# Hidden activations of an expert block: DRAM scratch and 32x32 turns on VectorE in place of transposes on TensorE

## The reference

```python
hid = jax.nn.silu(xb @ w1[e]) * (xb @ w3[e])   # xb: 128 rows of 1024, w1/w3: 1024 x 512
return hid @ w2[e]                             # w2: 512 x 1024
```

## Time and profile before

| | us |
|---|---|
| runs: median (lowest to highest of 3) | 1350.07 (1349.74 to 1353.28) |
| profiled execution: span from first to last instruction | 1348.3 |
| TensorE busy | 1311.4 |
| VectorE busy | 958.4 |
| GpSimd busy | 525.1 |
| ScalarE busy | 511.7 |

### The profile page before, as it was taken

One profiled execution on the slowest core, in us unless ns is written; L12 is line 12 of the kernel. 1 busy time (PEld: TensorE's weight loads), 2 busy tenths in 40 slices (PEclk: granted clock), 3 DMA queues, 4 the chain that ended last, 5 costly groups with the idle time before them and its releaser, 6 DMA issues. The chain is left out here.

```text
span 1348.3 us, 20368 instructions
## 1 busy us (share of the span) xinstructions
PE 1311.4 (97%) x6382; PEld 1095.8 (81%) x6383; DVE 958.4 (71%) x1357; ACT 511.7 (38%) x568; POOL 525.1 (39%) x543
## 2 busy tenths in 40 slices
PE   5999999999999999998999999999999999999995
PEld 5888888888888888887888888888888888888884
DVE  7758577687759785698777886665675677776564
ACT  3423234322443234323444454343443454434241
POOL 2001010111101110022566665755665656666555
PEclk9999999999999999999999999999999999999998
DMA  9625434563455344544777774563554545666421
GB/s 266 181 89 162 149 111 163 170 192 109 156 186 158 110 141 159 208 181 169 287 263 256 271 270 147 193 234 132 181 202 181 191 164 214 236 231 238 142 69 64
DMA packets 156522, 243.58 MB, mean 181 GB/s; under 512 B 18944, under 2 KB 84992, under 8 KB 156480
## 3 DMA queue, kind: packets, MB, share of 16 engines
q1 hardware_dynamic: 118624, 154.15, 35.3%
q0 software_dynamic: 28928, 71.74, 15.0%
q10 hardware_dynamic: 8928, 17.13, 3.7%
HBM read 211.97 MB, written 64.62 MB: 205 GB/s over the span
## 5 line engine op out<-in xcount | busy, mean ns | idle before, releaser
L520 PE MATMUL acc<-ring_hi 128*128 128x512 f32 (+1 forms) x800 | 308.8, 386 | 2.1 <-DVE ring_lo L1239 1.9
L522 PE MATMUL acc<-ring_hi,ring_lo 128*128 128x512 f32 (+1 forms) x800 | 305.6, 382 | 0.0
L521 PE MATMUL acc<-ring_lo,ring_hi 128*128 128x512 f32 (+1 forms) x800 | 305.3, 382 | 0.0
L520 PE MATMUL acc<-ring_hi,xt_hi 128*128 128x512 f32 x648 | 256.7, 396 | 4.1 <-issue 2.8
L522 PE MATMUL acc<-ring_hi,xt_lo 128*128 128x512 f32 x648 | 252.8, 390 | 0.0
L521 PE MATMUL acc<-ring_lo,xt_hi 128*128 128x512 f32 x648 | 252.4, 390 | 0.0
L1802 POOL TENSOR_TENSOR small<-small 128x1 f32<-128x1 f32 x31 | 47.4, 1527 | 360.8 <-DVE small L1208 360.8
L520 PEld LDWEIGHTS acc<-ring_hi 128*128 128x128 f32 x800 | 151.3, 189 | 30.1 <-DVE ring_lo L1239 2.5
L522 PEld LDWEIGHTS acc<-ring_hi,ring_lo 128*128 128x128 f32 x800 | 151.2, 189 | 29.1
L521 PEld LDWEIGHTS acc<-ring_lo,ring_hi 128*128 128x128 f32 x800 | 151.3, 189 | 27.7
L921 ACT CAST ring_hi<-stage_x 128x2048 fp32r<-128x2048 f32 x64 | 119.4, 1915 | 76.3 <-PE acc L522 75.8
(11 more groups left out here) (276 smaller groups left out, 1884.0 us busy)
## 6 DMA issues: line engine op xcount, KB each, us to landing
stage_x<-in_exp_w SPq DMA_DIRECT2D x64, 1024.0 KB, 6.2
stage<-in_w_in SPq DMA_DIRECT2D x64, 512.0 KB, 5.4
stage<-in_exp_w SPq DMA_DIRECT2D x32, 1024.0 KB, 6.6
stage<-in_w_out SPq DMA_DIRECT2D x32, 512.0 KB, 5.3
h_scratch<-hres POOLq DMA_DIRECT2D x16, 512.0 KB, 3.0
sum_scratch<-hres ACTq DMA_DIRECT2D x16, 512.0 KB, 2.9
hrow<-in_x POOLq DMA_DIRECT2D x12, 512.0 KB, 4.8
h_scratch<-hrow POOLq DMA_DIRECT2D x12, 512.0 KB, 3.0
```

Of the source, the lines that this page charges most:

```text
L520: nc.tensor.matmul(dst, w_hi, x_hi, start=start, stop=False)
L521: nc.tensor.matmul(dst, w_hi, x_lo, start=False, stop=False)
L522: return nc.tensor.matmul(dst, w_lo, x_hi, start=False, stop=stop)
```

## The change

`hid_tile` is no longer called for the blocks 1 to nb - 2; the first block and the last keep it. In its place `hid` goes to DRAM and comes back with the 32-column strips of its rows rearranged to partitions: quarter a of `hid_q` holds the columns 128a to 128a + 127 of all 128 rows, 32 rows on the partitions and four groups of rows side by side. VectorE's `transpose` then turns each 32x32 block of `hid_q` into `aux`. The partition 32a + c of slice k then holds column 128a + 32k + c, so w2 is loaded in that order of rows (`w2_v`), with four DMAs for each unit, and the first and the last block, which TensorE still transposes, write `hid` in the same order by four strided pieces (`by_tile`). ScalarE issues the store (`hid_out`) after `x_hi` and ahead of the w3 copies, and the four reads (`hid_back`) after them. `silu(b)` and `hid_hi(b - 1)` change places on ScalarE; VectorE's turn stands at the head of its block, ahead of `hid_lo`.

```diff
-    w2_v = exp_w2[0].rearrange("(g i) (k p) n -> i g p k n", p=P, g=NEG)
+    w2_v = exp_w2[0].rearrange("(g i) (a k c) n -> i g a c k n", a=QUARTERS, c=SUB, g=NEG)
+    hid_dram = nc.dram_tensor("hid_scratch", (P, DE), F32).ap()
+    hid_quarters = hid_dram.rearrange("(b r) (a f) -> a r b f", r=SUB, a=QUARTERS)
...
+                    for a in range(QUARTERS):
+                        src = w2_v[ex // NEG, ex % NEG, a, :, (j % 2) * 2:(j % 2 + 1) * 2, :]
+                        dst = staged(j)[a * SUB:(a + 1) * SUB, 0, :].rearrange("p (k c) -> p k c", k=2)
+                        sp.dma_start(dst, src).then_inc(s_stage[j], 16)
...
-            pe.wait_ge(s_plist, 1)
-            hid_tile(1)
...
                 down(pe_of)
-                hid_tile(b)
...
+            def hid_out(b):
+                act.wait_ge(s_hid, b + 1)
+                act.wait_ge(s_hq, b * 16 * QUARTERS)
+                act.dma_start(hid_dram, hid[:]).then_inc(s_hst, 16)
+            def hid_back(b):
+                act.wait_ge(s_hst, b * 16 + 16)
+                for a in range(QUARTERS):
+                    act.dma_start(hid_q[a * SUB:(a + 1) * SUB, :].rearrange("r (b f) -> r b f", f=P), hid_quarters[a])\
+                        .then_inc(s_hq, 16)
             def hid_hi(b):
-                act.wait_ge(s_htr, b + 1)
+                if isinstance(b, int) and b == 0:
+                    act.wait_ge(s_htr, 1)
+                else:
+                    act.wait_ge(s_hturn, b + 1)
...
+                    silu(b)
                     hid_hi(b - 1)
-                    silu(b)
...
                 x_hi(b + 1)
+                hid_out(b)
                 with act.If(ends > 0):
                     if first:
                         split_hi_expert(e_of + 1, 1)
                     units_hi(e_of + 1, 1)
+                hid_back(b)
...
-                if not (isinstance(b, int) and b == 0):
-                    dve.wait_ge(s_htr, b)
+                if isinstance(b, int) and b == 1:
+                    dve.wait_ge(s_htr, 1)
+                elif not (isinstance(b, int) and b == 0):
+                    dve.wait_ge(s_hst, b * 16)
...
+            def hid_turn(b):
+                dve.wait_ge(s_hq, b * 16 * QUARTERS)
+                V.transpose(aux[:].rearrange("p (k b c) -> p k b c", k=FT, c=SUB),
+                            hid_q[:].rearrange("p (b k c) -> p k b c", k=FT, c=SUB)).then_inc(s_hturn, 1)
...
-                    if split:
-                        hid_lo(b - 1)
+                    hid_turn(b)
+                    hid_lo(b - 1)
```

More of the change, by code:

```diff
@@ L64 @@
 ROW = D + NE
+SUB = 32
+QUARTERS = P // SUB
 ALIGN = 128
@@ L288, in build @@
         hid = e("hid", [P, DE])
+        hid_q = e("hid_q", [P, DE])
         ht_hi = e("ht_hi", [P, FT, P], F32R)
@@ L422, in build @@
         s_htr = sem("hid_transposed")
+        s_hst = sem("hid_rows_stored")
+        s_hq = sem("hid_quarters_in")
+        s_hturn = sem("hid_quarters_turned")
         s_hthi = sem("hid_t_hi")
@@ L491, in load_expert @@
             def load_expert(ex, j):
-                v = (w1_v, w3_v, w2_v)[j // 2]
-                kts = v.shape[3] // 2
-                src = v[ex // NEG, ex % NEG, :, (j % 2) * kts:(j % 2 + 1) * kts, :]
-                dst = staged(j)[:, 0, :].rearrange("p (k c) -> p k c", k=kts)
-                sp.dma_start(dst, src).then_inc(s_stage[j], 16)
+                if j < 4:
+                    v = (w1_v, w3_v)[j // 2]
+                    src = v[ex // NEG, ex % NEG, :, (j % 2) * 4:(j % 2 + 1) * 4, :]
+                    dst = staged(j)[:, 0, :].rearrange("p (k c) -> p k c", k=4)
+                    sp.dma_start(dst, src).then_inc(s_stage[j], 16)
[3 more added lines that the diff above has]
+                        dst = staged(j)[a * SUB:(a + 1) * SUB, 0, :].rearrange("p (k c) -> p k c", k=2)
+                        sp.dma_start(dst, src).then_inc(s_stage[j], 16)
             for j in (0, 1, 4, 2, 3, 5):
@@ L918, in split_hi_expert @@
             def split_hi_expert(ex, j):
-                act.wait_ge(s_stage[j], (ex + 1) * 16 + (MU // 2 * 32 if j < 2 else 0))
+                act.wait_ge(s_stage[j], (ex + 1) * (16 if j < 4 else 16 * QUARTERS) + (MU // 2 * 32 if j < 2 else 0))
                 nc.scalar.copy(ring_hi[:, j:j + 1, :], staged(j)).then_inc(s_ehi[j // 2], 1)
@@ L1160, in _ @@
                 act.wait_ge(s_ahout[t], 16 * NCH)
+            act.sem_inc(s_hst, 16)
+            act.sem_inc(s_hq, 16 * QUARTERS)
             silu(0)
@@ L1410, in route_hots @@
                                         lists[:, 0, 1:2], ALU.add).then_inc(s_gn, 1)
-                        hid_rows(0)
+                        hid_rows(0, True)
                     for t in range(TPC):
@@ L1571, in x_lo, with hid_rows @@
                                     ALU.subtract).then_inc(s_xtlo, 1)
-            def hid_rows(b):
+            def hid_rows(b, by_tile=False):
                 dve.wait_ge(s_silu, b + 1)
                 dve.wait_ge(s_w3, b + 1)
-                if not (isinstance(b, int) and b == 0):
-                    dve.wait_ge(s_htr, b)
+                if isinstance(b, int) and b == 1:
+                    dve.wait_ge(s_htr, 1)
+                elif not (isinstance(b, int) and b == 0):
+                    dve.wait_ge(s_hst, b * 16)
                 dve.wait_ge(s_gcol, b + 1)
                 col = gate_0 if isinstance(b, int) and b == 0 else gate[:, bass.ds(b, 1)]
-                V.scalar_tensor_tensor(out=hid[:], in0=act_a[:], scalar=col, in1=acc[1][:], op0=ALU.mult,
-                                       op1=ALU.mult).then_inc(s_hid, 1)
+                if by_tile:
+                    tiles = hid[:].rearrange("p (k a c) -> p a k c", k=FT, c=SUB)
+                    parts = [(tiles[:, a], *(t[:, a * P:(a + 1) * P].rearrange("p (k c) -> p k c", c=SUB)
+                                             for t in (act_a, acc[1]))) for a in range(QUARTERS)]
+                else:
+                    parts = [(hid[:], act_a[:], acc[1][:])]
+                for to, x_a, x_b in parts:
+                    ins = V.scalar_tensor_tensor(out=to, in0=x_a, scalar=col, in1=x_b, op0=ALU.mult, op1=ALU.mult)
+                ins.then_inc(s_hid, 1)
+            def hid_turn(b):
+                dve.wait_ge(s_hq, b * 16 * QUARTERS)
+                V.transpose(aux[:].rearrange("p (k b c) -> p k b c", k=FT, c=SUB),
+                            hid_q[:].rearrange("p (b k c) -> p k b c", k=FT, c=SUB)).then_inc(s_hturn, 1)
             def hid_lo(b):
@@ L1712, in final_last, with turn @@
                                        op0=ALU.mult, op1=ALU.add).then_inc(s_fo, 1)
-            def turn(b, first, split=True):
+            def turn(b, first):
                 e_of = dve.value_load(table[0:1, 0, bass.ds(b, 1)], min_val=0, max_val=NE - 1)
@@ L1729, in turn @@
                     units_lo(e_of + 1, 1)
-                if first:
-                    hid_lo(b)
                 final_sums(b - 1)
@@ L1739, in turn_last @@
                 ended = dve.value_load(table[0:1, 1, bass.ds(b - 1, 1)], min_val=0, max_val=1)
+                hid_turn(b)
                 hid_lo(b - 1)
-                hid_rows(b)
+                hid_rows(b, True)
                 dve.wait_ge(s_hthi, b + 1)
@@ L1750, in _ @@
             dve.wait_ge(s_elo[2], 2)
+            dve.sem_inc(s_hturn, 1)
             turn(1, True)
             nb1 = dve.value_load(nblocks[0:1, 1:2], min_val=NE, max_val=NB - 1)
-            turn(2, False, split=False)
-            with dve.Fori(3, nb1) as b:
+            with dve.Fori(2, nb1) as b:
                 turn(b, False)
```

4 lines of the change are left out of this document (2 added, 2 removed).

## The result

The changed kernel takes 1459.5 us as the median of 4 runs (1455.2 to 1464.5), the kernel before 1350.2 in the same comparison: ratio 1.081, 95% interval 1.079 to 1.082. The forecast was 1372 (1348 to 1388). The sign was right; the size was not: +109 us in place of +22.

A forecast was written before the change was run, and what follows sets the result against it. TensorE, busy 97% of the span, was taken to bound the kernel. Transposes saved -16.5, waits at expert changes +23.5, +12.8 and +2.0, strided pieces +0.4 gave +22.2 us: 1372 us, range 1348 to 1388.

The forecast's parts named there:

- order chain: VectorE's turn, then ScalarE's ht_hi, then ht_lo, 1.45 to 1.5 us later; +23.5, +12.8 and +2.0 us at expert changes.
- What the DMAs cost: Store and four reads of hid on ScalarE's queue each block: hidden with 2.2 us spare; strided hid pieces +0.4 us.
- the round trip through DRAM is late: Rival, 9%: reads of hid arrive too late in eight blocks before three-block changes, +20 us, 1391 us.
- (1): Sign on TensorE: 152 transposes fewer, and blocks without a change of expert 0.445 us shorter.
- (2): Sign on VectorE: the block turn from SBUF into PSUM takes near 0.75 us.
- (3): Sign: TensorE idle for xt_lo before a block's first matmul, about 1.7 us, six times.
- (4): Sign: TensorE idle for ht_lo before down, 2.4 us six times and 1.6 us eight times.
- (5): Sign: VectorE waits some 0.7 us for ht_hi in every block.
- (6): Sign: VectorE's turn does not wait for its reads of hid.
- The delays absorbed: Rival, 18% for half or more: VectorE's idle time ahead of ht_lo absorbs the delay; 1334 us, or 1353 if half.
- GpSimd and VectorE colliding: Rival, 13%: GpSimd's orow falls ahead of a VectorE split, 2.2 us at six changes, +13 us, 1384 us.
- The loop's end showing: Rival, 5%: TensorE's branch and table value at loop end needed the transposes as cover; saving nil, 1388 us.

The follow-up runs named there:

- turn_no_dma: Changed kernel without the store of hid and the four reads; VectorE's turn reads hid itself, and the wait for hid ahead of the store is gone: 1372.2 us.
- free_reads: Changed kernel with the four reads fetching another tensor's data in the same pieces, so ScalarE does not wait for the store: 1397.7 us.
- quarter_loads: Changed kernel with the weight loads of experts 1 to 15 bringing a quarter of their bytes; store, reads and waits stay: 1368.9 us.
- no_transpose: Kernel before without TensorE's 148 transposes of hid in the loop and nothing in their place: 1338.2 us.

## Why the forecast was wrong

*The ledger*, by medians: order chain without the store's place, less the saved slots, +22.0 (turn_no_dma); the five DMAs and the w3 copies held until `hid` is done, +25.5 (free_reads less that); ScalarE standing until the store has landed, with all that follows, the late reads and the late turn among it, +61.8 (the changed kernel less free_reads). Sum 109.3. The first equals what the forecast gave for the whole, but it is not the same sum of waits.

*The step that failed* is "What the DMAs cost": "store 0.33 and 2.9 (the landing of ScalarE's stores of twice the size) [...] Spare 2.2 us: hidden." Three things were wrong in it. The landing of 2.9 us came from stores of another stretch; in the loop the store meets SyncE's weight loads, and its median is 6.2 us. The reads meet them too: at the change shown, the turn starts 11.2 us after the first of them is issued (1012.60 to 1023.75), where the forecast had 1.4 for the issues and 4.7 for the landing. That SyncE reloads a weight buffer as soon as VectorE has split it, just ahead of `hid`, stands in the program, and I did not put the two side by side. Then the step asked only whether the data come in time for the turn, and not what stands on ScalarE behind an instruction that waits: `silu`, the w1 copies, `arow`, and through `arow` GpSimd's `out` and the next gather. "In a block without a change nothing on ScalarE is due then" is the wrong sentence. Last, the rival "the round trip through DRAM is late" had the right mechanism with 9%, and was priced at +20 as the turn's lateness alone, in eight blocks. How the +61.8 divide between the turn's lateness and the gather's isn't shown: free_reads shortens both, and in the changed kernel the two paths reach `down` within 2.5 us of each other at the 13 changes.

The Trainium skill ("DMA: Bandwidth & Descriptors", Issuing engines are not separate DMA queues) says that DMAs started by ScalarE, SyncE or GpSimd run on the same 16 engines and interleave; the runs agree: the same store takes 2.0 us in a quiet moment and up to 8.7 beside SyncE's loads, and 2.0 to 2.8 from its issue to the first read's throughout the loop with a quarter of their bytes. By the same page's fit for DMAs on GpSimd's path (Anatomy of one DMA: a fixed 2.0 us, and the bytes at 436 GB/s) a quiet 256 KB would take an estimated 2.6 us; the quiet store, which ScalarE issues, took 2.0.

*Point by point.* (1) 152 transposes fewer: right; the slots gave 14.9 us of 16.5. (2) The turn at 0.72 us: right; the estimate of 1.24 from the Trainium skill's figure was too high. (3) `xt_lo` 1.7 us six times: 1.33 to 1.37, right and a little large. (4) `ht_lo` 2.4 and 1.6 us: the mechanism is right where the loads are light (quarter_loads: 1.3 to 1.7 and 0.4 to 1.1, so mis-sized by about 0.9 us each); in the changed kernel a wait for the gather stands ahead of it and takes part of its place. At the loop's start, 2.0 in the forecast, `ht_lo` waits 8.5 us in the changed kernel, 5.5 in turn_no_dma and 3.8 in quarter_loads. (5) `ht_lo`'s wait of 0.7 us in each block: 0.79, right. (6) The turn not waiting for its reads: wrong, 93 us at 22 of 38.

*The +22 of turn_no_dma agrees by luck.* In spans, turn_no_dma stands 20.4 us over before: 14.9 less for the transposes, 28.2 more idle (65.1 against 36.9) and 7.1 of slower matmuls. The forecast had -16.5, +38.3 of waits and nothing for the clock. The waits came out a quarter smaller, and the clock filled a good part of that. They were other waits, too: 17.7 us for the gather, which the forecast didn't name, and next to none for `ht_lo` behind the changes. quarter_loads, which has the forecast's own waits, is the fairer test of the chain: +18.3 us over the 1350.6 before in its comparison, though with light loads.

*The clock.* The changed kernel and turn_no_dma have the same 6230 instructions on TensorE, and these are busy 1339.5 and 1303.6 us. So 35.9 of the 89.0 us between the two spans are not waits but the same matmuls running slower, most of it, by the granted clock, at the lower level after waits, and 53.1 are idle. In turn_no_dma the waits at the changes are 2.1 us at most and the mean clock is 0.992; in the changed kernel they are 3.5 to 4.8 for the gather alone, with 0.2 to 2.3 more for `ht_lo` soon after, and it is 0.959. Where the gaps are short, 28.2 us more of idle come with 7.1 of slower matmuls (turn_no_dma against the kernel before, whose transposes are deducted); where they are long, 53.1 more come with 35.9. A run that sets the length of the gaps alone was not made.

*Other rivals.* The delays absorbed: false. GpSimd and VectorE colliding: not as priced, since the w1 splits take 2.29 us each in place of 2.74; but GpSimd's side of it is there at every change with a wait, where `orow` takes 3.8 to 3.9 us and the copies ahead of the gather up to 2.26 (above), and it delays the gather. The loop's end showing: false, by no_transpose. What stays open is how the 25.5 us divide over the store's place and the traffic, and the 61.8 over the gather and the turn.

## What to carry to other kernels

A wait for a DMA on a compute engine's queue is priced by everything queued behind it, and not only by whether the data come in time: write down that list, follow it over the next engines to the bottleneck, and only then say "hidden". Take a DMA's landing time from a row with the same neighbours in flight, since the same 256 KB took 2.0 us alone and 8.7 beside bulk loads that another engine had issued. Before calling a run "the rest without X", look for the waits that went with X: here the DMA's removal also took a semaphore wait that the forecast had counted. And where a change makes TensorE wait for several us at a time, add the lower clock behind each wait; here 53 us of waiting came with 36 of slower matmuls.

## What the runs showed of the hardware that I had not expected

- The block turn of 128x512 float32 from SBUF into PSUM takes 0.72 to 0.73 us on VectorE, the same as an elementwise operation of that size (0.69 to 0.74).
- One issue on ScalarE's queue took from 0.31 to 1.01 us (four reads: median 0.45), and 0.67 in a row of fifteen. The cost of issuing is not fixed, and many small DMAs hold the engine longer than one wait.
- After a standstill of 4.25 us and one of 1.66 TensorE ran at 0.52 of its full clock for about 5 us; in turn_no_dma, whose waits at the changes are 2.1 us at most, the mean clock is 0.992.
- A 256 KB store on one queue is held up by loads on another: it was longest, 8.1 to 8.8 us to the first read's issue, behind eight pieces of 256 KB, and 6.2 to 7.3 behind two loads of 1 MB. Holding the w1 loads back for about 7 us brought its median landing from 6.2 to 4.4 us and the kernel 38 us.
- GpSimd's copies of 128x1 numbers took up to 2.26 us beside a split on VectorE, and 0.18 to 0.19 beside none; the gather is queued behind them.
